# Projections ahead of the gate and score matmuls in each step of a latent-attention pipeline, and squares ahead of the exponential

## The reference, cut to what matters

```python
    q = split_heads(rms_norm(c_q, mla_cq_norm) @ mla_w_uq, MLA_HEADS)
    kv = split_heads(rms_norm(c_kv, mla_ckv_norm) @ mla_w_ukv, MLA_HEADS)
    k_nope, v = jnp.split(kv, [MLA_NOPE_DIM], axis=-1)
    k_rope_h = jnp.broadcast_to(k_rope[:, None], (B, MLA_HEADS, L, MLA_ROPE_DIM))
    k = jnp.concatenate([k_nope, k_rope_h], axis=-1)
    q = rms_norm(q, mla_q_norm)
    k = rms_norm(k, mla_k_norm)
    ...
    q = jnp.concatenate([q[..., :MLA_NOPE_DIM], rope(q[..., MLA_NOPE_DIM:], cos, sin)], axis=-1)
    k = jnp.concatenate([k[..., :MLA_NOPE_DIM], rope(k[..., MLA_NOPE_DIM:], cos, sin)], axis=-1)
    o_mla = merge_heads(block_causal_attention(q, k, v)) @ w_branch_mla

    g_fox, g_mla = jnp.split(jax.nn.sigmoid(gate_logit + b_gate), N_BRANCH, axis=-1)
    return (g_fox * o_fox + g_mla * o_mla) @ w_out
```

## Time and profile before

| | us |
|---|---|
| median of 3 runs | 2540.45 |
| lowest and highest run | 2538.03, 2544.03 |
| the profiled execution | 2538.03 |
| its span in the trace | 2536.2 |
| TensorE busy in the span | 2379.9 |
| mean granted TensorE clock | 0.971 |

### The profile page before, as it was taken

How to read it: one execution, slowest core, us unless ns; L and a number is a source line. 1 busy time by engine, 2 the same in 40 slices (tenths; PEclk the granted TensorE clock), 3 DMA queues, 4 the chain that set the end, 5 groups by cost and what they waited for, 6 DMA issues and landing times. The chain is left out here.

```text
span 2536.2 us, 36868 instructions
## 1 busy us (share of the span) xinstructions
PE 2379.9 (94%) x14060; PEld 2106.2 (83%) x14060; DVE 1426.0 (56%) x2052; ACT 959.9 (38%) x1619; POOL 513.7 (20%) x634
## 2 busy tenths in 40 slices
PE   6899999999968999988999999989989999999999
PEld 6899999999968878866777777778877888887887
DVE  7665555565554575562555555554276666556553
ACT  5333323343334444542343433353343333334332
POOL 0033300000022442340233333332410332000000
PEclk8999999999989999989999999999999999999999
DMA  5366633475321000010111111023614656427553
GB/s 187 124 208 207 206 117 105 155 275 186 131 84 51 26 4 23 1 34 23 41 37 45 42 37 37 30 98 132 239 52 134 226 192 213 139 68 276 207 200 109
DMA packets 132698, 297.99 MB, mean 117 GB/s; under 512 B 10096, under 2 KB 57072, under 8 KB 129216
## 3 DMA queue, kind: packets, MB, share of 16 engines
q1 hardware_dynamic: 132544, 295.88, 33.7%
HBM read 206.99 MB, written 88.72 MB: 117 GB/s over the span
## 5 line engine op out<-in xcount | busy, mean ns | idle before, releaser
L1070 DVE TENSOR_TENSOR f_w_lo<-f_rw,f_w_hi 128x1024 fp32r<-128x1024 f32 x154 | 194.6, 1264 | 220.6 <-ACT f_w_hi L590 220.6
L833 PE MATMUL f_ps<-u_hi,f_w_hi 128*128 128x260 f32 (+1 forms) x1056 | 283.4, 323 | 25.9 <-DVE f_w_lo L1070 13.2
L833 PE MATMUL f_ps<-u_hi,f_w_lo 128*128 128x260 f32 (+1 forms) x1056 | 282.6, 322 | 0.0
L833 PE MATMUL f_ps<-u_lo,f_w_hi 128*128 128x260 f32 (+1 forms) x1056 | 282.3, 322 | 0.0
L590 ACT CAST f_w_hi<-f_rw 128x1024 fp32r<-128x1024 f32 x154 | 161.3, 1047 | 164.2 <-PE f_ps L833 157.0
L833 PE MATMUL f_ps<-f_far_hi,f_w_hi 128*128 128x260 f32 (+1 forms) x792 | 211.5, 321 | 8.7 <-DVE f_ev L1086 8.7
L833 PEld LDWEIGHTS f_ps<-u_hi,f_w_hi 128*128 128x128 f32 x1056 | 178.0, 192 | 42.0 <-DVE f_w_lo L1070 14.5
L833 PE MATMUL f_ps<-f_far_lo,f_w_hi 128*128 128x260 f32 (+1 forms) x792 | 210.7, 321 | 0.0
L833 PE MATMUL f_ps<-f_far_hi,f_w_lo 128*128 128x260 f32 (+1 forms) x792 | 210.7, 320 | 0.0
L833 PEld LDWEIGHTS f_ps<-u_lo,f_w_hi 128*128 128x128 f32 x1056 | 177.5, 191 | 14.4
L833 PEld LDWEIGHTS f_ps<-u_hi,f_w_lo 128*128 128x128 f32 x1056 | 177.2, 191 | 14.1
(11 more groups left out here) (394 smaller groups left out, 5926.6 us busy)
## 6 DMA issues: line engine op xcount, KB each, us to landing
f_rw<-in_gu SPq DMA_DIRECT2D x88, 512.0 KB, 4.2
f_rw<-kept_dsum SPq DMA_DIRECT2D x32, 704.0 KB, 4.5
f_rw<-kept_hid SPq DMA_DIRECT2D x33, 520.0 KB, 5.6
f_rw<-in_down SPq DMA_DIRECT2D x24, 704.0 KB, 4.1
f_rw<-kept_hid SPq DMA_DIRECT2D x33, 512.0 KB, 5.5
h_in<-in_wd SPq DMA_DIRECT2D x11, 1024.0 KB, 6.7
kept_dsum<-h_in SPq DMA_DIRECT2D x44, 256.0 KB, 3.2
h_out<-in_wd SPq DMA_DIRECT2D x11, 1024.0 KB, 7.1
```

What stands on the lines that cost most here:

```text
L833: last = nc.tensor.matmul(out[:, b, 0:N], w[:, c], u[:, b * N:(b + 1) * N], start=(j < 3 and k == 0 and i == 0), stop=(k == 3 and i == 2), ...
L1070: nc.vector.tensor_tensor(slot(w_lo, st), src, slot(w_hi, st).bitcast(F32), ALU.subtract).then_inc(wlo_done, 1)
```

## The change

Two moves, in the preparation and in every head that has a successor. On ScalarE the square of unit w is made in `early`, ahead of the copy of the logits and of the exponential of step w; it was behind the exponential. On TensorE the products of unit w are the first thing in step w, ahead of the maxima, the gates and the scores; they were behind the scores (in the first preparation behind the first gates). The waits are the same as before, each with its instruction.

```diff
@@ -2322,8 +2322,6 @@
                     if u == 0:
                         upto(act, st_ready, NW, p, h - 1, 0)
                     nc.scalar.copy(split_of(h, u)[0][0:DK, t0:t0 + n], x32[0:DK, u % 2, 0:n]).then_inc(xhi_done, 1)
-
-            def square(p, h, w):
                 if w < NU:
                     is_q, c = units[w]
                     t0, n = QK_TOKENS[c]
@@ -2393,7 +2391,6 @@
                         copy_logits(p, h + 1, w)
                     exponential(p, h, w)
                     if more:
-                        square(p, h + 1, w)
                         late(p, h + 1, w)
                         gate_weights(p, h + 1, w, more=next_gate)
                     if w == FINISH_0:
@@ -2410,7 +2407,6 @@
             for w in range(NW):
                 early(0, 0, w)
                 copy_logits(0, 0, w)
-                square(0, 0, w)
                 late(0, 0, w)
                 gate_weights(0, 0, w)
             over_pairs(act, pair)
@@ -2560,12 +2556,12 @@
 
             def head(p, h, more=True):
                 for w in range(NW):
+                    if more and w < NU:
+                        products(p, h + 1, w)
                     if more:
                         maxima(p, h + 1, w, 0)
                         gates(p, h + 1, w, 0)
                     scores(p, h, w)
-                    if more and w < NU:
-                        products(p, h + 1, w)
                     if more:
                         maxima(p, h + 1, w, 1)
                         gates(p, h + 1, w, 1)
@@ -2578,10 +2574,10 @@
                 head(p, 0)
                 head(p, 1, more=not last)
             for w in range(NW):
+                if w < NU:
+                    products(0, 0, w)
                 maxima(0, 0, w, 0)
                 gates(0, 0, w, 0)
-                if w < NU:
-                    products(0, 0, w)
                 maxima(0, 0, w, 1)
                 gates(0, 0, w, 1)
                 prepare(0, 0, w)
```

## The result

| | before | changed |
|---|---|---|
| median, us (4 runs each) | 2542.05 | 2612.48 |
| lowest and highest | 2538.03, 2544.03 | 2605.61, 2620.97 |
| ratio, 95% interval | | 1.0281 (1.0246 to 1.0316) |
| profiled execution | 2538.03 | 2614.54 |
| its span | 2536.2 | 2612.7 |

The change costs 70 us by the medians and 76.5 us between the two profiled spans. The forecast was 2596, with a range up to 2612.0. The direction and most of the mechanism were right; the size was too small, and the median lies just outside the range.

The account below looks back on a forecast made before the run. TensorE was taken as the bound, its products already waiting for VectorE's scaling. To 2538 us came 35 (cover), 2.8 (first preparation), 2.5 (logits' copy), minus 2.5 (DMA) and 20 (clock): 2596, range 2570 to 2612.

Parts of the forecast that it names:

- What bounds the kernel, and that the latency keeps its length: Latent attention: TensorE bounds, working 51.2 of 54 us a head; the products start as late after the broadcast as before.
- 60 to 63 instead of 54: Expected length in us of one latent attention head after the change, about 5 of it without the clock.
- Lost cover, 5.0 us a head, 35 us: Steps 2 to 5 of seven heads: gates and scores now run after the products' wait; 35 us, upper end 41.
- The first preparation, 2.8 us: Head prepared before any scores run: one gate group of 0.69 us lost as cover, four times.
- The logits' copy, 0.25 us a head: Step 3: gates wait for ScalarE's copy behind the square; with 0.7 in the first, 2.5 us, bounds 0 and 5.
- To have the square earlier brings nothing: ScalarE's squares ahead of the exponential: no gain, as the square was late only once, 0.3 us in all.
- The DMA of the maxima, minus 2.5: Step 0: products now stand ahead of the score matmul that waits for this DMA, in seven heads; saves 2.5 us.
- The clock, 20 us and at most 27: TensorE's clock falls to 1.2 GHz behind 12 of 16 long waits, 1.7 us each; bounds 0 and 27.
- four waits of the fox attention: Line 1908, four pairs: clock 0.77 behind two waits of 1.82 us, 1.00 behind two of at most 1.68.
- falls behind the short waits too: Rival: TensorE's clock falls behind short waits as well, 32 times, 54 us, giving 2630 us; chance 0.08.

Follow-up runs that it names:

- the filler: Changed kernel plus 5 (q) or 7 (k) useless 512-column matmuls ahead of the products in steps 2 to 5, none in first preparation: 2578.3 us, 1.0141.

## Why the prediction was wrong

- *What bounds the kernel, and that the latency keeps its length*: right. The products start as long behind the broadcast as before, and the waits came out as 1.5 and 2.0 to 2.1, as worked out from the starts. One reading was off: the 54 us of the earlier trace rows are not a whole head. From one transposed maxima to the next the seven heads take 57.9 to 59.6 us, and 65.6 to 72.7 in the changed kernel, so the "60 to 63 instead of 54" has the wrong base. The sum doesn't use it.
- *Lost cover, 5.0 us a head, 35 us*: right. With the clock held at 1.00 by the filler the seven heads cost 33.8 us, and without it the idle time grew by 31.4.
- *The first preparation, 2.8 us*: right for the waits for `mla_x`, which grew by 2.7 us, and the logits' copy added the 0.7. Left out was that the products of step 0 now run in the wait at the entry of the stage, and wait there only for the weights' DMA. The first row is of the kernel before, the second of the changed one:

```profile
PE mla_bank L73 <- DVE mla_gate_lo L2679: 8.3, 1, 8.3
```

```profile
PE mla_bank L2431 <- DMA mla_w_head<-in_mla: 5.1, 1, 5.1
```

  That gives most of it back, and with the two falls of the clock the preparation costs 3.1 us.
- *The logits' copy, 0.25 us a head*: about right where the clock stays at 1.00, with 3.4 us of waits in the filled kernel against 2.0. In the changed kernel it is 0.9; that the matmuls ahead of the wait, slowed by the clock, hide the copy is a likely reason, but not tested. The squares' move without the products' move costs 12 us, through this very copy. "To have the square earlier brings nothing" was right; that it costs little was right only for the two moves together.
- *The DMA of the maxima, minus 2.5*: wrong, there was nothing to gain. The 3.0 us of the earlier trace rows are waits of weight loads. In the seven heads before, the matmuls idled there for 0.12 us at most, and the 0.7 us of the last head, which has no products, are still there. In the sum it had been set against the logits' copy, so its error stays within 2.5 us.
- *The clock, 20 us and at most 27*: this step failed. The clock fell 17 times in the seven heads and cost 39 us of full-speed work there, 34.6 of it in longer busy time; two more falls are in the first preparation. The forecast had 12 falls of 16 long waits at 1.7 us each, and none behind the waits of 1.5. For the long waits alone that was about right: with only those left, 9 falls in 14 waits cost 20 us. The nothing for the short waits was wrong: with only those left, 11 falls cost 19 us. It rested on four waits of the fox attention, which were read as a limit between 1.68 and 1.82 us. Four cases, two each way and about 90 us apart, showed that such waits can go both ways, and not where a limit lies or what waits that return in every step do. The rival "falls behind the short waits too" (2630) had the mechanism right and the count too high: it had 32 falls, and the profiled time lies about halfway between it and the forecast.
- Not wrong but left out: a fall can last longer than the 1.7 us of loss that was taken for each. The 17 falls cost 2.3 us each on average. Equal heads lost from 0.03 to 0.14 of the clock.

The range was too narrow at the top for the same reason: 27 us for the clock was the bound of the chosen reading, not the bound of what was unknown.

## What to carry to other kernels

Ahead of an instruction that waits for a latency, count the independent work between what starts the latency and that instruction; moving it forward past this work costs the whole of it, as soon as it waits at all. On a busy TensorE, look for the clock behind added waits that come back in every step. Here waits of 1.5 and 2.1 us cost about twice their length (31.4 us more idle time, 66.0 us more in all), and matmuls of no use in the gap told the two halves apart. And when an operation is moved within its engine's list, look at what it is moved past (here the logits' copy) and who waits for that.

## What the runs showed of the hardware

In all seven heads before, waits of TensorE of 1.0 us and less left the clock at 1.00. Waits of 1.5 us alone, with none above 0.5 beside them, brought it to 0.96, those of 2.1 alone to 0.96, and both to 0.92. Two shorter waits close together did it too (0.99 us and then 1.04 for the logits' copy, 0.98 over the heads). Equal waits in equal heads did and did not do it, so a single head says little. The Trainium skill, page "TensorE: Matmul & The Clock Gate", section "HAM oscillation — how this bites in real kernels", explains such falls by idle stretches between bursts. The filler, which took 32 us off seven heads with 168 added matmuls, agrees with that cause. The length that the section asks of such a stretch is above every wait in these heads, so by it the clock would have stayed; here the measurement decides.
